# Nine places instead of eight for the expert weights, and smaller edits to keep-alive products and waits on TensorE

## The reference

```python
# first block, per layer: adaptive scale and shift, then the mixer
mod = silu(c) @ w_ada[i] + b_ada[i]
h = rms_norm(x) * (1 + sc1) + sh1
y = short_conv(h) or neighbourhood_attention(h, hc) @ w_out     # "aout"
# second block
merged = sigmoid(gate_a) * (o_attn @ w_branch_attn) + sigmoid(gate_r) * (o_rwkv @ w_branch_rwkv)
h = h + gt1 * (merged @ w_out)                                  # "wout"
# mixture of experts, two experts of 32 per token
for wg, wu, wd, cw in experts:
    hdn = silu(xt @ wg) * (xt @ wu)
    acc = acc + cw[:, None] * (hdn @ wd)
h = h + gt2 * acc
```

## Time and profile before

| what | us |
|---|---|
| median of 3 runs | 1930.22 (1929.96 to 1930.50) |
| the profiled execution, its own time | 1930.59 |
| its span in the trace | 1928.9 |
| PE busy | 1741.1 (90%) |
| DVE busy | 879.8 (46%) |
| ACT busy | 258.4 (13%) |
| POOL busy | 401.9 (21%) |
| DMA, mean over the span | 218 GB/s |
| tiles of expert weights | 96 transfers of 2048 KB |

### The profile page before, as it was taken

One profiled execution on the slowest core, in us unless ns is written; L12 is line 12 of the kernel. 1 busy time (PEld: TensorE's weight loads), 2 busy tenths in 40 slices (PEclk: granted clock), 3 DMA queues, 4 the chain that ended last, 5 costly groups with the idle time before them and its releaser, 6 DMA issues.

```text
span 1928.9 us, 25634 instructions
## 1 busy us (share of the span) xinstructions
PE 1741.1 (90%) x10864; PEld 1275.2 (66%) x10864; DVE 879.8 (46%) x1405; ACT 258.4 (13%) x563; POOL 401.9 (21%) x331
## 2 busy tenths in 40 slices
PE   5999999999999999999999999999999666675666
PEld 3888478888888878768888888778786122221222
DVE  3899568888883355672435114565223000000001
ACT  2000020000000121271000012251202000000000
POOL 1553045555642239000111011300000000000000
PEclk9999999999999999999999999999999788877788
DMA  9453335544441340025975470420075999999997
GB/s 397 144 218 110 109 133 173 174 158 161 157 186 60 131 197 1 30 100 212 388 248 202 153 284 6 191 78 25 3 312 233 428 428 428 428 429 428 427 429 320
DMA packets 49661, 420.45 MB, mean 218 GB/s; under 512 B 5536, under 2 KB 5936, under 8 KB 23312
## 3 DMA queue, kind: packets, MB, share of 16 engines
q1 hardware_dynamic: 30240, 345.27, 44.2%
q0 software_dynamic: 18880, 71.16, 10.8%
q10 hardware_dynamic: 432, 2.43, 0.3%
HBM read 417.79 MB, written 1.05 MB: 217 GB/s over the span
## 4 chain that ended last, share of the span: by engine, by line
PE 67%; DMA 22%; DVE 6%; issue 2%; ACT 1%; POOL 0%; SPq 0%; ACTq 0%; DVEq 0%; POOLq 0%
DMA ring<-w_moe 21%; PE PS L1246 8%; PE PS L1213 8%; PE PS L1174 7%; PE PS L1256 7%; PE PS L1325 6%; PE PS L1697 4%; PE PS L1647 4%; PE PS L1308 4%; DVE SC L2058 3%; PE PS L1347 3%; PE PS L1491 2%; PE PS L1976 1%; DMA ring<-w_ada 1%; PE PS L1625 1%
## 5 line engine op out<-in xcount | busy, mean ns | idle before, releaser
L1491 PE MATMUL PS<-ring,A 128*32 128x512 f32 x768 | 124.0, 780 | 87.0 <-DMA ring<-w_moe 86.2
L2058 DVE SCALAR_TENSOR_TENSOR SC<-A,CS,SC 128x512 f32<-128x512 f32 x208 | 165.8, 851 | 11.9 <-DMA A<-ada 9.8
L1246 PE MATMUL PS<-A,ring 128*128 128x256 f32 x704 | 154.6, 380 | 0.3 <-ACT A L722 0.3
L1213 PE MATMUL PS<-ring 128*128 128x256 f32 x672 | 150.9, 380 | 0.0
L1491 PEld LDWEIGHTS PS<-ring,A 128*32 128x32 f32 x768 | 24.7, 126 | 186.9 <-DMA ring<-w_moe 139.7
L1246 PEld LDWEIGHTS PS<-A,ring 128*128 128x128 f32 x704 | 132.9, 190 | 20.3 <-issue 2.6
L1213 PEld LDWEIGHTS PS<-ring 128*128 128x128 f32 x672 | 126.9, 190 | 20.7 <-issue 3.9
L2332 DVE TENSOR_TENSOR A<-A,PS 128x512 f32<-128x512 f32 x8 | 5.5, 689 | 289.9 <-ACT A L820 289.9
L1325 PE MATMUL PS<-A,ring 128*128 128x256 f32 (+1 forms) x384 | 111.7, 451 | 1.8 <-DVE A L2717 1.3
L1213 PE MATMUL PS<-A,ring 128*128 128x256 f32 x504 | 112.3, 379 | 0.0
L527 POOL DMA_DIRECT2D ring<-ada x64 | 34.8, 544 | 359.8 <-DVE SC L2058 238.6
(11 more groups left out here) (421 smaller groups left out, 2668.6 us busy)
## 6 DMA issues: line engine op xcount, KB each, us to landing
ring<-w_moe SPq DMA_DIRECT2D x72, 2048.0 KB, 35.7
A<-w_moe SPq DMA_DIRECT2D x24, 2048.0 KB, 35.3
ring<-w_fin SPq DMA_DIRECT2D x44, 1024.0 KB, 6.6
ring<-ada POOLq DMA_DIRECT2D x64, 512.0 KB, 4.4
A<-ada POOLq DMA_DIRECT2D x64, 512.0 KB, 4.4
ring<-w_fout SPq DMA_DIRECT2D x16, 1408.0 KB, 7.5
ring<-w_conv SPq DMA_DIRECT2D x12, 1024.0 KB, 16.2
ring<-w_qkv SPq DMA_DIRECT2D x6, 2048.0 KB, 16.1
```

What stands on the lines that cost most here:

```text
L1213: mm = pe.matmul(PS[:, bank, half * 256:half * 256 + 256], left[:, k], right[:, k], start=(k == 0), stop=(k == 3))
L1246: mm = pe.matmul(PS[:, 2 * (s % 3) + half, 0:SEQ], slot("fin1", s, k * 256 + half * 128, k * 256 + half * 128 + 128), h_of(k, SEQ), start= ...
L1491: mm = pe.matmul(PS[CAP * e:CAP * (e + 1), g, :], XG[:, k * P + e * CAP:k * P + (e + 1) * CAP], expert_slot(j + k, w, w + 512), start=(k = ...
L2058: ins = dve.scalar_tensor_tensor(out=ACC[:, i, :], in0=w, scalar=scale, in1=ACC[:, i, :], op0=ALU.mult, op1=ALU.add)
```

## The change

1. The experts get a ninth place, `A[:, 14592:18688]`, sixth in order and free at `merged` = 8. The small tensors that lay there move: `XG` and `YS` to `X`, `PTS` to the front of `A`, `HF`, `SGF`, `HTT`, `LG` and `LT` behind the new place. The loops of SP and TensorE go by trips of three turns (36 tiles, 4 times round 9 places), with the first and the last turn outside.
2. The second half of gathered tokens goes to bank 3 and not 1. The first four tiles of a turn wait only for the first half of `XG`; `down` waits for both halves of the next `XG`. The second of two weighted placement tables is made inside the first turn (`weighted(1)`), since both now share `YS`.
3. In the last turn `keep_on(2, 4)` stands ahead of tiles 2 to 7 of gate/up and `keep_on(1, 4)` ahead of each of the four down tiles.
4. At the start `norm_spread(0)` goes ahead of `ada_first(2)`, `keep_on(4, 4)` comes in ahead of `ada_first(3)`, and `keep_on(4, 6)` behind `ada_columns` becomes `keep_on(4, 2)`.
5. In sparse attention `keep_on(5, 3)` comes in between the first two turns.
6. "aout" waits for `o_na` term by term in its first tile. "wout" waits for 7 merged pieces ahead of its first term, and for the eighth ahead of its last.

```diff
-MOE_LANDED = (0, 1, 2, 8, 9, 5, 3, 4)
+MOE_LANDED = (0, 1, 2, 8, 9, 10, 5, 3, 4)
+MOE_PLACES = 9
...
-        XG, HF, YS = A[:, 16896:17920], A[:, 17920:18432], A[:, 18432:19456]
-        SGF, HTT = A[:, 19456:19968], A[:, 19968:20480]
+        XG, HF, YS = X[:, 3072:4096], A[:, 18688:19200], X[:, 2048:3072]
+        SGF, HTT = A[:, 19200:19712], A[:, 19712:20224]
...
         MOE_BUF = [ring[:, 0:4096], ring[:, 4096:8192], ring[:, 8192:12288], A[:, 4096:8192], A[:, 10496:14592],
-                   ring[:, 20480:24576], ring[:, 12288:16384], ring[:, 16384:20480]]
+                   A[:, 14592:18688], ring[:, 20480:24576], ring[:, 12288:16384], ring[:, 16384:20480]]
...
-            for i in range(8):
+            for i in range(MOE_PLACES):
...
-            for i in range(8, 24):
-                expert_used(0, i - 8)
+            for i in range(MOE_PLACES, MOE_SLOTS):
+                expert_used(0, i - MOE_PLACES)
                 expert_load(0, i)
-            with sp.Fori(1, NGR // 2) as pair:
-                for i in range(24):
-                    expert_used(pair, i - 8)
-                    expert_load(pair, i)
+            with sp.Fori(0, 2) as trip:
+                for i in range(MOE_SLOTS, MOE_SLOTS + 36):
+                    expert_used(trip, i - MOE_PLACES)
+                    expert_load(trip, i)
+            for i in range(96 - MOE_SLOTS, 96):
+                expert_used(0, i - MOE_PLACES)
+                expert_load(0, i)
...
+                        if stage == "aout" and m == 0:
+                            pe.wait_ge(sem("o_na"), k + 1)
+                        if stage == "wout" and m == 0 and k in (0, KD - 1):
+                            pe.wait_ge(sem("merged"), KD if k else KD - 1)
...
                     turn(2 * p)
+                    if p == 0:
+                        keep_on(5, 3)
                     turn(2 * p + 1)
...
-                            mm = pe.matmul(PS[:, 2 - half, (c % 4) * P:(c % 4) * P + P], XT[:, t, c * P:(c + 1) * P],
+                            mm = pe.matmul(PS[:, 2 + half, (c % 4) * P:(c % 4) * P + P], XT[:, t, c * P:(c + 1) * P],
...
                     pe.wait_ge(sem("xg_act"), it + 1)
-                    pe.wait_ge(sem("xg_dve"), it + 1)
                     for k in range(KD):
-                        expert_landed(pe, j + k, pair)
+                        if k == 4:
+                            pe.wait_ge(sem("xg_dve"), it + 1)
+                        if last and k >= 2:
+                            if k == 2:
+                                pe.wait_ge(sem("ys_act"), it)
+                                pe.wait_ge(sem("ys_dve"), it)
+                            keep_on(2, 4)
+                        expert_landed(pe, j + k, trip)
...
                     if not last:
                         pe.wait_ge(sem("xg_act"), it + 2)
+                        pe.wait_ge(sem("xg_dve"), it + 2)
                     for q in range(4):
-                        expert_landed(pe, j + 8 + q, pair)
+                        if last:
+                            keep_on(1, 4)
+                        expert_landed(pe, j + 8 + q, trip)
...
             ada_first(1)
+            norm_spread(0)
             ada_first(2)
-            norm_spread(0)
+            keep_on(4, 4)
             ada_first(3)
             ada_columns()
-            keep_on(4, 6)
+            keep_on(4, 2)
...
-            pe.wait_ge(sem("o_na"), 8)
             out_proj("aout", lambda k: O1[:, k * SEQ:(k + 1) * SEQ], SEQ)
...
-            pe.wait_ge(sem("merged"), KD)
             out_proj("wout", lambda k: MG[:, k * SEQ:(k + 1) * SEQ], SEQ)
...
                     if first:
+                        dve.wait_ge(sem("pt_mm"), 2)
+                        weighted(1)
```

More of the change, by code:

```diff
@@ L1479, in down, with turn @@
                     return mm
-                def turn(pair, even, first=False, last=False):
-                    it = pair * 2 + (0 if even else 1)
-                    j = 0 if even else MOE_SLOTS
+                def turn(trip, n, first=False, last=False):
+                    it = trip * 3 + n
+                    j = n * MOE_SLOTS
                     pe.wait_ge(sem("xg_act"), it + 1)
-                    pe.wait_ge(sem("xg_dve"), it + 1)
                     for k in range(KD):
-                        expert_landed(pe, j + k, pair)
+                        if k == 4:
[6 more added lines that the diff above has]
+                        expert_landed(pe, j + k, trip)
                         for g in range(2):
@@ L1527, in pe_gathered @@
                 gather(0, 1)
-                turn(0, True, first=True)
-                turn(0, False)
-                with pe.Fori(1, NGR // 2 - 1) as pair:
-                    turn(pair, True)
-                    turn(pair, False)
-                turn(NGR // 2 - 1, True)
-                turn(NGR // 2 - 1, False, last=True)
+                turn(0, 0, first=True)
+                with pe.Fori(0, 2) as trip:
+                    for n in range(1, 4):
+                        turn(trip, n)
+                turn(0, NGR - 1, last=True)
                 pe.wait_ge(sem("ys_act"), NGR)
@@ L1546, in pe_dense, with turn @@
                     pe.matmul(PS[:, 4 + b, :], ident, CT0, start=True, stop=True)
-                def turn(pair, even):
-                    it = pair * 2 + (0 if even else 1)
-                    j = 0 if even else MOE_SLOTS
+                def turn(trip, n):
+                    it = trip * 3 + n
+                    j = n * MOE_SLOTS
                     def gate_up(e, q):
@@ L1593, in turn @@
                     mm.then_inc(sem("dn_mm"), 1)
-                with pe.Fori(0, NGR // 2) as pair:
-                    turn(pair, True)
-                    turn(pair, False)
+                turn(0, 0)
+                with pe.Fori(0, 2) as trip:
+                    for n in range(1, 4):
+                        turn(trip, n)
+                turn(0, NGR - 1)
             pe.wait_ge(sem("zeros"), 2)
@@ L2341, in turn, with weighted @@
                     dve.tensor_copy(YS[:, 512:1024], PS[:, 3, :]).then_inc(sem("ys_dve"), 1)
+                def weighted(t):
+                    dve.tensor_tensor(YS.rearrange("p (e s) -> p e s", e=NE), PG[:, t, :].rearrange("p (e s) -> p e s", e=NE),
+                                      CMB[:, t, :].unsqueeze(2).to_broadcast([P, NE, CAP]), ALU.mult).then_inc(
+                        sem("pcw_made"), 1)
                 for t in range(2):
@@ L2346, in dve_gathered @@
                 dve.wait_ge(sem("xt_mm"), 4)
-                for t in range(2):
-                    dve.tensor_tensor(PCW[t].rearrange("p (e s) -> p e s", e=NE),
-                                      PG[:, t, :].rearrange("p (e s) -> p e s", e=NE),
-                                      CMB[:, t, :].unsqueeze(2).to_broadcast([P, NE, CAP]), ALU.mult).then_inc(
-                        sem("pcw_made"), 1)
+                weighted(0)
                 turn(0, first=True)
```

52 lines of the change are left out of this document (25 added, 27 removed).

## The result

| | before | changed |
|---|---|---|
| median of 5 runs, us | 1929.96 | 1917.89 |
| lowest and highest | 1928.95, 1930.50 | 1916.69, 1920.53 |
| the profiled execution, own time | 1930.59 | 1916.69 |
| its span | 1928.9 | 1915.0 |

The ratio is 0.9941, with an interval of 0.9927 to 0.9956: 12 us faster, where 11.85 were summed up and 1918.4 forecast. The profiled execution of the changed kernel is the lowest of its five runs, so the two traces are 13.9 us apart, 1.8 more than the medians. That has to be explained too.

The account below looks back on a forecast made before the run. TensorE sets the pace up to the experts, weight transfers at 428 GB/s within them. 4.9 + 0.65 + 1.3 + 0.5 + 1.3 + 0 + 1.5 + 1.7 = 11.85 us gives a median of 1918.4, range 1916.0 to 1922.2.

Parts of the forecast that it names:

- The ninth place: Expert weight loads: one more tile lands in the transfer pause ahead of the first used tile, 4.9 us earlier; bounds 0 and 4.9.
- The prediction's sum for the stream: Expert loads before the change: from 1481.12, 88 tiles at 4.90 us make 431 us, the last landing at about 1917.1.
- The start of the experts: First expert product no longer waits for ACT's copy of the second half of gathered tokens: 0.65 us earlier; bounds 0 and 0.73.
- New waits in a turn: Expert turns: waits of `down` and for the second placement table are hidden by the transfers, costed at nothing.
- "wout" and "aout": Output projections: TensorE's idle time ahead of them vanishes, 1.3 us at "wout" and 0.5 us at "aout".
- The queue of products at the start: Ahead of the first convolution product: two keep-alive products instead of six let it start 1.3 us earlier; bounds 0 and 1.35.
- The clock at the start: Fourth adaptive slot: a remaining pause of 2.8 us can still take the clock, so 0 us counted.
- the rival: Fourth adaptive slot: the clock holds at the start, 1.65 us more gained, 1916.8 us; chance 0.2.
- Sparse attention: Between the first two turns: three products fill TensorE's wait and keep the clock for the gate products, 1.5 us; bounds -1.0 and 1.8.
- The last turn: Last expert turn: added products keep full clock for the last tile and scatter, 1.7 us; bounds -1.5 and 1.7.
- The slower rival: Last turn: products stay at clock 0.50, 6.9 us a place against 4.89 between landings, 1940 us; chance 0.02.

## Why the prediction was right

It held as a whole: 1917.89 against 1918.4, inside 1916.0 to 1922.2. The terms as measured come to about 11.7 us, without the clock at the start; that the sum is so near to 11.85 is in part luck, since three small misses upwards (0.15 to 0.2 each) stand against one of 0.6 downwards. Only the ninth place, and the two output projections less surely, show in medians; the other terms rest on distances in single traces. Step by step:

- **The ninth place**, 4.9 us: 4.89 in the traces, 5.0 by holding one load back. The mechanism is the one stated, a load moved into the pause; slack in the stream later on is worth nothing. The prediction's sum for the stream is off by one tile's time: 1481.1 + 431 us gives 1912.3 and not 1917.1. From the first load behind the pause to TensorE's start on the last tile it is 436.0 us before and 431.1 changed, 4.8 us over 88 and 87 tiles at 4.90 us in both, so this drops out of the gain.
- **The start of the experts**, 0.65: 0.8 by taking it back. The idle time was 0.73, which I had as the upper bound; the first product also began 0.07 us closer to the gather.
- **New waits in a turn**, 0: TensorE was held for 1.92 us in turn 0, and the distance to the last tile did not grow.
- **"wout" and "aout"**, 1.3 and 0.5: 1.39 and 0.62 come back when the waits do. The stretch that ends at "wout" shows 1.73 between the two profiles; the profiles with the new wait differ there by as much as 1.4 (159.36 to 160.76), and with the old wait put back it is 162.03, so where the remaining 0.4 comes from stays open.
- **The queue of products at the start**, 1.3: 1.1 and 1.4 in two variants.
- **The clock at the start.** I took 0, by the fall at 1249, and gave the rival 0.2. Between the two profiles the slot shows 1.64 us, the rival's number; the pause was 2.07 us and not 2.8, as the eight records began 0.17 us later and took 1.99 us and not 1.74, and the slot came 0.32 us earlier. But what failed is the frame of both: each took the fall to be a property of the program's order. Both profiles of the kernel before have it, yet with the old order put back into the changed kernel the slot was at full clock in two of two, and without the four products in one of one. So the order alone doesn't decide it, and the row at 30.65 doesn't speak for every execution. Whether the four products keep it from falling stays open. The prediction also put the four products at no cost; in one of nine profiles they held the fourth slot back by about 1.5 us. The Trainium skill (TensorE: Matmul & The Clock Gate, "What's actually happening") says that the chip judges activity on a clock of its own that doesn't start with the kernel. The traces fit that: over 14 profiles the first fall of the granted clock comes at 24.5, 24.9, 25.0 (twice), 25.5, 26.0, 26.2, 30.5, 30.6 or 36.2 us, or (in four) not before the experts; the unaltered changed kernel had none in one profile and two in the other, at 25.0 and 1264.1. Had I drawn on it, the two would have been one case with a chance, and not a forecast and a rival.
- **Sparse attention**, 1.5 with a bound of 1.8: 1.7, in three executions of four.
- **The last turn**, 1.7 with a bound of -1.5: 1.1 net. The two parts came as summed (2.69 to 1.92, and 2.05 to 1.17, together 1.65), and the stores took 0.5 us of it back: from the first update to the end it is 7.1 us before and 7.6 after, and the slowest of the four stores took 3.7 us from issue to landing where it took 3.2 before (3.2 in the second profile of the kernel before as well, 3.3 to 4.0 in all others). Why they land later stays open. The 10.1 us that the prediction named for this stretch are 10.66 for that reason. That the added products are done just in time held to 0.22 us.
- **The slower rival.** With four products it didn't come near. With eight it came, at full clock: 5.51 us a tile against 4.89, and the gain was gone. That TensorE can become the bound of this turn was right; the condition named for it, the lower clock, was not tested.

The profiled pair differs by 1.8 us more than the medians because the profile of before lies 0.6 us over its median and that of the changed kernel 1.2 under its own. The fall at the fourth slot, 1.64 us of the pair's difference, isn't shown to be that excess, since the second profile of the kernel before has it too. The second profile of the changed kernel is 1.65 us longer than the first by other places: 0.53 us at the start, where the slot came later, and 1.12 behind attention, where the clock fell.

## What to carry to other kernels

Where a transfer-bound stage follows a pause of its queue, count the loads that fit into the pause: here the further place that fitted was worth one whole transfer, once, and as slack behind a saturated queue nothing. A wait ahead of an accumulation can be moved to the term that needs it, and is then covered by the terms ahead. Products that only keep the clock up belong in waits that they fit, at the lower clock and behind late work too; before costing one, look at more than one profile, since a fall of the clock in a given place need not come in the next execution; and ahead of a stage that waits for transfers check that tile and filler together stay under the time of one transfer.

## What the runs showed of the hardware that was not expected

- The granted clock fell at different places in executions of nearly the same program: at 30.6 and 30.5 us (the kernel before), at 25.0 and 26.2 (the old start; the new start without its four products), at 36.2 (two variants with the new start, one of them with a fall at 26.0 as well), or not at all before the experts (the changed kernel's first profile and three variants). The 16 records of the fourth slot took 1.90 us, or 3.33 and 3.54, by it.
- One pause of 1.61 us among short transposes goes with a fall at sparse attention in three of four profiles; with six records of filler in it there is none in that place in ten of ten.
- Products meant to keep the clock up can land in a stretch of half clock themselves: four of them took 3.00 us instead of 1.99 and, behind a slow third slot, held the fourth back by about 1.5 us.
- Two executions of one unaltered kernel on one chip can be 6 us apart (the kernel before, 1927.11 to 1933.42 in 11 runs), more than the two falls ahead of the experts in its one trace there cost (1.4 and 1.7 us). Where the rest comes from stays open.
